# Permuting partitions for a rotary embedding: eight on-chip DMA copies in place of four matrix products

## The chip, the core and the metric

The kernel runs on one NeuronCore of a Trainium2 chip. Its engines are TensorE (PE, with its weight loads as PEld), VectorE (DVE), ScalarE (ACT), GpSimd (POOL) and SyncE (SP). SP only issues DMA transfers here; ACT issues some as well. The metric is the device time of one execution in microseconds (us), taken as the median of several runs.

## The reference, cut to what matters

One layer of a decoder trunk: a normalised input is projected once, the columns of the projection go to four token mixers (A: RWKV-7, B: HGRN2, C: RetNet-style retention, D: RG-LRU), and their outputs are gated, merged and projected back. The change is in branch C, in the rotary embedding of its queries and keys, for 1024 tokens and four heads of 32 channels:

```python
def _rope(t, cos, sin):
    t1, t2 = jnp.split(t, 2, -1)
    return jnp.concatenate([t1 * cos - t2 * sin, t1 * sin + t2 * cos], -1)

def _retention(q, k, v, norm_g):
    ...
    q = _rope(q.astype(jnp.float32).reshape(B, T, H, Dk), cos, sin)
    k = _rope(k.astype(jnp.float32).reshape(B, T, H, Dk), cos, sin) * (Dk ** -0.5)
```

Within a head's 32 channels the first 16 need the second 16 and the other way round. The kernel keeps channels on partitions and tokens along the free dimension, so this is a swap of neighbouring groups of 16 partitions, with a sign.

## The kernel before

The projection is 59 column tiles of 128 columns, in the order of the list `BULK`: four tiles of D, seven of A, then branch C's tiles CQ, CK, CV, CV+1, CG, CG+1, and so on. A tile is computed in split precision: each 128x128 block of weights and each half of 512 tokens takes three products (`hn_hi*w_hi`, `hn_lo*w_hi`, `hn_hi*w_lo`, L591). A tile has two weight halves `p` (0 and 1) and two token halves, so 48 products in four parts of twelve.

Every engine's program is written by hand and runs in order; semaphores tie the engines together. Five places matter.

- **SP (L426 to L449)** loads the weights of tile `bi`, half `p`, into `w_raw[p]` when POOL has split that half of the tile before it (the wait on `s_w_lo_ready`). Its instructions go out strictly in order.
- **POOL (L498 to L509)** splits `w_raw[p]` into `w_hi[p]` and `w_lo[p]`: a cast (L506) and a subtraction (L508). For half 1 of a tile it first waits until PE has finished the tile before.
- **PE (L774 to L813)** runs the tiles. Behind the tile CK (number 12 of `BULK`, counted from 0) come the four products with the table `perm` (L805), a 128x128 signed permutation: q = 0 is the query in `slot(20)`, q = 1 the key in `slot(21)`, each in two token halves, into four PSUM banks. Then come tile 13, the first half of tile 14, and `head_sums(18, 0)` (L797), four products with a block matrix of ones that sum squares over a head for branch A. Ahead of these PE waits for `s_kz_ready`.
- **ACT** copies each finished tile from PSUM to its slot (L1216), and issues the loads of the cosine and sine tables into `slot(16)` and `slot(17)` (L1287, L1288).
- **DVE (L1726 to L1749)** does the rotation: for each of the four 128x512 pieces the permuted piece times sine from PSUM (L1731), the piece itself times cosine in place (L1734), and their sum (L1736). Then it scales the key by a table of decays into `slot(17)` (L1745), which raises `s_kz_ready`, and the query into `slot(16)` (L1748).

```python
            pe.wait_ge(s_gates_ready, 16)
            for q in range(2):
                pe.wait_ge(s_evac, 2 * (BULK_AT[CQ + q] + 1))
                for n in range(2):
                    mm(bank[4 + 2 * q + n][:, :], tb("perm"), ...).then_inc(s_rot_done, 1)
            project(1)
            project_part(0)
            project_part(1)
            pe.wait_ge(s_kz_ready, 1)
            head_sums(18, 0)
```

The wait on `s_kz_ready` is there because the banks 4 to 7 that `head_sums` writes are those that DVE reads in the rotation.

Of the kernel before, what the change touches and what calls it, by code (L numbers as in the profile page):

```python
# [32 lines left out]
P = 128  # L33
T = 1024
# [22 lines left out]
TABLES = (("ident", 128), ("blockones", 128), ("perm", 128), ("xi", 128), ("zeta", 128), ("decay", 512),  # L57
# [42 lines left out]
def build(nc, ins, out_d):  # L100
    x_d, w_mod_d, w_in_d, w_branch_d, w_out_d = (ins[n] for n in ("x", "w_mod", "w_in", "w_branch", "w_out"))
    with ExitStack() as ctx:
# [3 lines left out]
        def sem(name):  # L106
            return ctx.enter_context(nc.semaphore(name))
# [3 lines left out]
        def after(s):  # L111

            counts[s.name] = counts.get(s.name, 0) + 1
            return counts[s.name]
# [48 lines left out]
        s_rot_done = sem("rot_done")  # L163
# [111 lines left out]
        def slot(i):  # L275

            return slots[:, i, :]
# [15 lines left out]
        def tb(name):  # L297
            a, b = TCOL[name]
            return tab[:, a:b]

        def st(a, n):
            return stage[:, a:a + n]
# [21 lines left out]
        rope_tmp = [st(1024, HALF), st(1536, HALF)]  # L324
# [5 lines left out]
        spent = tab[:, TCOL["perm"][0]:TCOL["decay"][1]]  # L330
# [77 lines left out]
        def _(sp):  # L408
# [18 lines left out]
            for bi, ct in enumerate(BULK):  # L427
                if bi < FIRST:
                    continue
                if bi == FIRST:  # L430
                    for src, dst in ((ins["tables"][:, P:], tab[:, P:]), (ins["wa2"], wa2[:, :]),
                                     (ins["reset64"], reset)):
                        sp.dma_start(dst, src).then_inc(s_tables_landed, 16)
                    sp.wait_ge(s_lru_w_zero, 1)
                    for g, name in enumerate(("lru_wa", "lru_wx")):
                        for q in range(4):
                            j, r = q // 2, slice(64 * (q % 2), 64 * (q % 2) + 64)
                            sp.dma_start(lru_w[r, 2 * g + j, r], ins[name][0, q, :, :]).then_inc(
                                s_lru_w_landed, 16)
                for p in range(2):  # L440
# [106 lines left out]
        def _(pe):  # L547
# [254 lines left out]
            for q in range(2):  # L802
                pe.wait_ge(s_evac, 2 * (BULK_AT[CQ + q] + 1))
                for n in range(2):
                    mm(bank[4 + 2 * q + n][:, :], tb("perm"), slot(20 + q)[:, n * HALF:(n + 1) * HALF],  # L805
                       start=True, stop=True).then_inc(s_rot_done, 1)
# [718 lines left out]
        def _(dve):  # L1525
# [5 lines left out]
            def halves(n):  # L1531
                return slice(n * HALF, (n + 1) * HALF)
# [193 lines left out]
            dve.wait_ge(s_rope_landed, 32)  # L1726
            for q in range(2):
                for n in range(2):
                    dve.wait_ge(s_rot_done, 2 * q + n + 1)
                    s = slot(20 + q)[:, halves(n)]  # L1730
                    nc.vector.tensor_tensor(rope_tmp[n], bank[4 + 2 * q + n][:, :], slot(17)[:, halves(n)], MUL)\  # L1731
                        .then_inc(s_vector_step, 1)
                    dve.wait_ge(s_vector_step, after(s_vector_step))
                    nc.vector.tensor_tensor(s, s, slot(16)[:, halves(n)], MUL).then_inc(s_vector_step, 1)  # L1734
                    dve.wait_ge(s_vector_step, after(s_vector_step))
                    nc.vector.tensor_tensor(s, s, rope_tmp[n], ADD).then_inc(s_vector_step, 1)  # L1736
                    dve.wait_ge(s_vector_step, after(s_vector_step))
# [422 lines left out]
def shape_tables():  # L2160
# [6 lines left out]
    perm = np.zeros((P, P))  # L2167
    for m in range(P):
        if m % 32 < 16:
            perm[m + 16, m] = -1  # L2170
        else:
            perm[m - 16, m] = 1
    t["perm"] = perm
# [24 lines left out]
    return {"tables": tables, "cos": np.cos(ang).astype(f), "sin": np.sin(ang).astype(f),  # L2198
# [36 lines left out]
```

## Time and profile before

| | before |
|---|---|
| median of 3 runs | 1105.72 us |
| the three runs | 1106.65, 1105.67, 1105.72 us |
| span of the profiled execution | 1106.6 us |
| PE busy | 1075.6 us (97%) |
| DVE busy | 595.6 us (54%) |
| POOL busy | 375.6 us (34%) |
| ACT busy | 319.9 us (29%) |
| mean granted TensorE clock | 0.996 |

The span is from the first to the last instruction of the profiled execution; of the three runs the 1106.65 us stands next to it, 0.05 us above, and that is what lies around the span. A busy share is an average over stages. The rotation stands at 199 to 218 us of the span, in the stage in which PE streams projection tiles without a pause.

### The profile page before, as it was taken

To read this page: it belongs to the slowest core of one execution; us is meant where nothing else is said; L and a number is where in the kernel's file an instruction comes from. 1 tells how busy PE (TensorE), PEld (TensorE's weight loads), DVE (VectorE), ACT (ScalarE), POOL (GpSimd) and SP (SyncE) were. 2 spreads that over 40 slices of the span, in tenths; PEclk is the share of its full clock that TensorE was granted. 3 is DMA by queue.
4 is the path that set the end of the run, shared out by engine and by line. 5 is a ranking of instruction groups with operands and counts; after the bars stand their busy time and mean duration, and the time that the engine had idled before them with its cause. 6 is when DMAs were issued, how large, how long until landed. Compare 5 with 4: busy or idle time off the path is not lost.

```text
span 1106.6 us, 23043 instructions
## 1 busy us (share of the span) xinstructions
PE 1075.6 (97%) x9992; PEld 830.4 (75%) x9992; DVE 595.6 (54%) x1068; ACT 319.9 (29%) x533; POOL 375.6 (34%) x343
## 2 busy tenths in 40 slices
PE   7999999999999999999999999999999999999997
PEld 5686787767677777777777786877878777887885
DVE  3768933986555332343443118647778587423543
ACT  4545113321521221221221033144545341001221
POOL 1431533312356312212212233244434239762000
PEclk9999999999999999999999999999999999999999
DMA  9700111200100101101111021120101126412221
GB/s 352 259 20 9 48 50 47 76 29 24 40 26 26 49 25 35 40 25 36 37 29 31 28 68 33 44 58 26 50 25 37 39 68 242 143 39 95 95 76 58
DMA packets 80133, 70.28 MB, mean 64 GB/s; under 512 B 4128, under 2 KB 68896, under 8 KB 80032
## 3 DMA queue, kind: packets, MB, share of 16 engines
q1 hardware_dynamic: 74560, 49.34, 14.3%
q10 hardware_dynamic: 5472, 19.47, 4.8%
q8 instruction: 79, 1.29, 0.5%
q14 instruction: 22, 0.18, 0.1%
HBM read 64.60 MB, written 4.19 MB: 62 GB/s over the span
## 4 chain that ended last, share of the span: by engine, by line
PE 88%; DVE 7%; POOL 2%; DMA 1%; ACT 1%; issue 1%; SPq 1%; DVEq 0%; ACTq 0%; POOLq 0%
PE bank L591 53%; PE bank L1104 8%; PE bank L640 8%; PE bank L692 2%; PE bank L1059 1%; DVE slots L1678 1%; PE bank L919 1%; PE bank L915 1%; DMA slots<-in_w_mod 1%; PE bank L797 1%; PE bank L861 1%; PE bank L884 1%; DVE slots L1662 1%; PE bank L972 1%; POOL y_lo L477 1%
## 5 line engine op out<-in xcount | busy, mean ns | idle before, releaser
L591 PE MATMUL bank<-hn_hi,w_hi 128*128 128x512 f32 x880 | 363.0, 412 | 5.8 <-ACT slots L1216 2.3
L591 PE MATMUL bank<-hn_lo,w_hi 128*128 128x512 f32 x880 | 344.4, 391 | 0.0
L591 PE MATMUL bank<-hn_hi,w_lo 128*128 128x512 f32 x880 | 343.8, 391 | 0.0
L506 POOL CAST w_hi<-w_raw 128x512 fp32r<-128x512 f32 x110 | 87.0, 791 | 556.6 <-PE bank L591 556.6
L591 PEld LDWEIGHTS bank<-hn_hi,w_hi 128*128 128x128 f32 x880 | 165.3, 188 | 47.7 <-issue 6.9
L591 PEld LDWEIGHTS bank<-hn_hi,w_lo 128*128 128x128 f32 x880 | 165.6, 188 | 36.4
L591 PEld LDWEIGHTS bank<-hn_lo,w_hi 128*128 128x128 f32 x880 | 165.8, 188 | 32.0 <-issue 1.9
L508 POOL TENSOR_TENSOR w_lo<-w_raw,w_hi 128x512 fp32r<-128x512 f32 x110 | 156.2, 1420 | 8.8
L1238 ACT ACTIVATE stage<-bank 128x512 f32<-128x512 f32 x64 | 37.2, 598 | 160.8 <-PE bank L591 141.9
L1216 ACT ACTIVATE slots<-bank 128x512 f32<-128x512 f32 x42 | 24.6, 598 | 123.0 <-PE bank L591 123.0
L1837 DVE TENSOR_TENSOR stage<-stage,bank 128x512 f32<-128x512 f32 x48 | 33.0, 687 | 49.8 <-PE bank L640 48.6
L640 PE MATMUL bank<-y_hi,w_branch_hi 128*128 128x512 f32 x128 | 53.8, 421 | 0.0
L640 PE MATMUL bank<-y_hi,w_branch_lo 128*128 128x512 f32 x128 | 50.7, 396 | 0.0
L640 PE MATMUL bank<-y_lo,w_branch_hi 128*128 128x512 f32 x128 | 50.5, 395 | 0.0
L1104 PE MATMUL bank<-out_w_hi,hn_hi 128*128 128x512 f32 x128 | 49.9, 390 | 0.2 <-DVE hn_lo L2125 0.2
L1104 PE MATMUL bank<-out_w_lo,hn_hi 128*128 128x512 f32 x128 | 49.8, 389 | 0.0
L1104 PE MATMUL bank<-out_w_hi,hn_lo 128*128 128x512 f32 x128 | 49.8, 389 | 0.0
L1839 DVE TENSOR_TENSOR slots<-slots,stage 128x512 f32<-128x512 f32 x48 | 41.5, 865 | 1.7
L2141 DVE TENSOR_TENSOR fin_tmp<-bank,slots 128x512 f32<-128x512 f32 x16 | 11.1, 692 | 38.2 <-PE bank L1104 38.1
L1924 DVE TENSOR_TENSOR stage<-stage,bank 128x128 f32<-128x128 f32 x32 | 9.2, 287 | 40.5 <-PE bank L919 40.2
L1911 DVE TENSOR_TENSOR stage<-bank,tab 128x128 f32<-128x128 f32 x32 | 9.3, 292 | 38.0 <-PE bank L915 38.0
L518 POOL TENSOR_TENSOR w_branch_lo<-w_branch,w_branch_hi 128x256 fp32r<-128x256 f32 x32 | 28.1, 877 | 2.6
(329 smaller groups left out, 1604.9 us busy)
## 6 DMA issues: line engine op xcount, KB each, us to landing
w_raw<-in_w_in SPq DMA_DIRECT2D x110, 256.0 KB, 2.8
slots<-in_w_mod SPq DMA_DIRECT2D x16, 512.0 KB, 11.4
slots<-in_x SPq DMA_DIRECT2D x8, 512.0 KB, 9.6
w_branch<-in_w_branch SPq DMA_DIRECT2D x32, 128.0 KB, 2.6
slots<-in_w_mod ACTq DMA_DIRECT2D x8, 512.0 KB, 5.4
slots<-in_w_out ACTq DMA_DIRECT2D x8, 512.0 KB, 6.3
xr<-in_x ACTq DMA_DIRECT2D x8, 512.0 KB, 3.5
out<-xr ACTq DMA_DIRECT2D x8, 512.0 KB, 2.6
```

What stands on the lines that cost most here:

```text
L506: nc.gpsimd.tensor_copy(w_hi[p][:, :, :], w_raw[p][:, :, :]).then_inc(s_pool_step, 1)
L508: nc.gpsimd.tensor_tensor(w_lo[p][:, :, :], w_raw[p][:, :, :], w_hi[p][:, :, :].bitcast(F32), ALU.subtract).then_inc(s_w_lo_ready, 1)
L518: nc.gpsimd.tensor_tensor(w_branch_lo[h][:, :, :], w_branch[h][:, :, :], w_branch_hi[h][:, :, :].bitcast(F32), ALU.subtract)\
L591: last = mm(o, w[p][:, k4, :], h[:, k, n * HALF:(n + 1) * HALF], start=(p == 0 and k4 == 0 and q == 0), stop=(p == 1 and k4 == 3 and q == 2))
L640: last = mm(o, w[:, k, :], h[:, k, :], start=(k == 0 and q == 0), stop=(k == 1 and q == 2))
L692: last = mm(bank[q][:, :], w[p][:, k4, cols], h[:, k, n * HALF:(n + 1) * HALF], start=(k == 0 and z == 0), stop=(k == KT - 1 and z == 2))
L1104: last = mm(bank[(2 * tt + n) % 8][:, :], m[tt % 2][:, k * P:(k + 1) * P], w[k][:, n * HALF:(n + 1) * HALF], start=(k == 2 and q == 0), st ...
L1216: nc.scalar.activation(slot(PROJ[ct])[:, halves(n)], src, ACT.Silu if ct in GATED else ACT.Copy).then_inc(s_evac, 1)
L1238: nc.scalar.activation(sig[n], bank[(6 if mi == AHEAD else 0) + n][:, :], ACT.Sigmoid).then_inc(s_evac, 1)
L1837: nc.vector.tensor_tensor(sig[n], sig[n], bank[(4 if mi == AHEAD else 2) + n][:, :], MUL).then_inc(s_vector_step, 1)
L1839: nc.vector.tensor_tensor(o, o, sig[n], ADD).then_inc(s_merged, 1)
L2141: nc.vector.tensor_tensor(tmp, bank[(2 * i + n) % 8][:, :], slot(2)[:, halves(n)], MUL)\
```

## The change

The four products with `perm` and the table itself are gone. In their place SP copies the two slots 20 and 21 within the on-chip memory to a new buffer `rotated` (128 x 2 x 1024, in `stage`), with eight DMA copies of 16 partitions each, 128 KB apiece: group `g` of 16 partitions gets what group `g ^ 1` holds. The copies stand in SP's program ahead of the weight loads of tile 15 and wait until tile CK has been copied out of PSUM. The sign moves into the sine table, on the host. DVE waits for all eight copies (`s_rot_landed` at 128) and then works on whole rows of 1024: six instructions of 128x1024 from on-chip memory in place of twelve of 128x512, four of which read PSUM. `head_sums` still waits for `s_kz_ready`.

```diff
@@ SP
+                if bi == BULK_AT[CK] + 3:
+                    sp.wait_ge(s_evac, 2 * (BULK_AT[CK] + 1))
+                    for g in range(8):
+                        src = slice(16 * (g ^ 1), 16 * (g ^ 1) + 16)
+                        sp.dma_start(rotated[16 * g:16 * g + 16, :, :], slots[src, 20:22, :]).then_inc(s_rot_landed, 16)
                 for p in range(2):
                     if bi > FIRST:
                         sp.wait_ge(s_w_lo_ready, 2 * (bi - FIRST) + p - 1)
@@ PE
             pe.wait_ge(s_gates_ready, 16)
-            for q in range(2):
-                pe.wait_ge(s_evac, 2 * (BULK_AT[CQ + q] + 1))
-                for n in range(2):
-                    mm(bank[4 + 2 * q + n][:, :], tb("perm"), slot(20 + q)[:, n * HALF:(n + 1) * HALF],
-                       start=True, stop=True).then_inc(s_rot_done, 1)
             project(1)
@@ DVE
             dve.wait_ge(s_rope_landed, 32)
+            dve.wait_ge(s_rot_landed, 128)
             for q in range(2):
-                for n in range(2):
-                    dve.wait_ge(s_rot_done, 2 * q + n + 1)
-                    s = slot(20 + q)[:, halves(n)]
-                    nc.vector.tensor_tensor(rope_tmp[n], bank[4 + 2 * q + n][:, :], slot(17)[:, halves(n)], MUL)\
-                        .then_inc(s_vector_step, 1)
-                    dve.wait_ge(s_vector_step, after(s_vector_step))
-                    nc.vector.tensor_tensor(s, s, slot(16)[:, halves(n)], MUL).then_inc(s_vector_step, 1)
-                    dve.wait_ge(s_vector_step, after(s_vector_step))
-                    nc.vector.tensor_tensor(s, s, rope_tmp[n], ADD).then_inc(s_vector_step, 1)
-                    dve.wait_ge(s_vector_step, after(s_vector_step))
+                s, turned = slot(20 + q), rotated[:, q, :]
+                nc.vector.tensor_tensor(turned, turned, slot(17), MUL).then_inc(s_vector_step, 1)
+                after(s_vector_step)
+                nc.vector.tensor_tensor(s, s, slot(16), MUL).then_inc(s_vector_step, 1)
+                dve.wait_ge(s_vector_step, after(s_vector_step))
+                nc.vector.tensor_tensor(s, s, turned, ADD).then_inc(s_vector_step, 1)
+                dve.wait_ge(s_vector_step, after(s_vector_step))
@@ host tables
-    perm = np.zeros((P, P))
...
-    t["perm"] = perm
-    return {"tables": tables, "cos": np.cos(ang).astype(f), "sin": np.sin(ang).astype(f),
+    return {"tables": tables, "cos": np.cos(ang).astype(f), "sin": (np.sin(ang) * np.where(p % 32 < 16, -1, 1)[:, None]).astype(f),
```

SP's program before, from the first weight load of the tile loop to the first load of a branch matrix. `w_raw` is the buffer of a half tile; the 26 loads in one row are those of tiles 5 to 17, two for each.

```order
L438 DMA lru_w<-in_lru_wx 64x64 x4
L448 DMA w_raw<-in_w_in 128x4x128 [waits w4_ready]
L448 DMA w_raw<-in_w_in 128x4x128 [waits gains_ready,w4_ready]
L448 DMA w_raw<-in_w_in 128x4x128 [waits w_lo_ready] x26
L455 DMA w_branch<-in_w_branch 128x2x128
```

The same place of SP's program in the changed kernel (`stage<-slots` are the copies into `rotated`, rows of 2048 elements):

```order
L438 DMA lru_w<-in_lru_wx 64x64 x4
L453 DMA w_raw<-in_w_in 128x4x128 [waits w4_ready]
L453 DMA w_raw<-in_w_in 128x4x128 [waits gains_ready,w4_ready]
L453 DMA w_raw<-in_w_in 128x4x128 [waits w_lo_ready] x20
L444 DMA stage<-slots 16x2048 [waits evac]
L444 DMA stage<-slots 16x2048 x7
L453 DMA w_raw<-in_w_in 128x4x128 [waits w_lo_ready] x6
L460 DMA w_branch<-in_w_branch 128x2x128
```

Twenty loads, those of tiles 5 to 14, stand ahead of the copies; the last of them is half 1 of tile 14. Behind the copies come the loads of tiles 15 to 17.

DVE's program before, from the end of branch A's preparation (L1724) to the query's scaling (L1748):

```order
L1724 COPY slots<-slots 128x1024 [waits vector_step]
L1731 TENSOR_TENSOR stage<-bank,slots 128x512 [waits rot_done,rope_landed,a_b_ready]
L1734 TENSOR_TENSOR slots<-slots 128x512 [waits vector_step]
L1736 TENSOR_TENSOR slots<-slots,stage 128x512 [waits vector_step]
L1731 TENSOR_TENSOR stage<-bank,slots 128x512 [waits rot_done,vector_step]
...
L1745 TENSOR_TENSOR slots<-slots,tab 128x1024 [waits vector_step]
L1748 TENSOR_TENSOR slots<-slots,tab 128x1024 [waits kz_ready]
```

And in the changed kernel:

```order
L1724 COPY slots<-slots 128x1024 [waits vector_step]
L1730 TENSOR_TENSOR stage<-stage,slots 128x1024 [waits rot_landed,rope_landed,a_b_ready]
L1732 TENSOR_TENSOR slots<-slots 128x1024
L1734 TENSOR_TENSOR slots<-slots,stage 128x1024 [waits vector_step]
L1730 TENSOR_TENSOR stage<-stage,slots 128x1024 [waits vector_step]
L1732 TENSOR_TENSOR slots<-slots 128x1024
L1734 TENSOR_TENSOR slots<-slots,stage 128x1024 [waits vector_step]
L1743 TENSOR_TENSOR slots<-slots,tab 128x1024 [waits kz_ready]
```

The first multiplication of the rotation now waits for the copies (`rot_landed`) where it waited for a product of PE (`rot_done`); nothing else has changed its place in DVE's queue.

## Rows read from the trace of the kernel before

**Rows 1.** The page: busy time of each engine, and the chain by engine.

```profile
PE 1075.6 (97%) x9992; PEld 830.4 (75%) x9992; DVE 595.6 (54%) x1068; ACT 319.9 (29%) x533; POOL 375.6 (34%) x343
...
PE 88%; DVE 7%; POOL 2%; DMA 1%; ACT 1%; issue 1%; SPq 1%; DVEq 0%; ACTq 0%; POOLq 0%
```

**Rows 2.** Timeline, PE, around the products with perm: start us, us, engine, line, operation, tiles.

```profile
198.84 0.39 PE L591 MATMUL bank<-hn_hi,w_lo 128*128 128x512 f32 x1
199.06 3.59 PE L805 MATMUL bank<-slots,tab 128*128 128x512 f32 x8
202.09 0.79 PE L591 MATMUL bank<-hn_hi,w_hi 128*128 128x512 f32 x1
202.73 0.39 PE L591 MATMUL bank<-hn_lo,w_hi 128*128 128x512 f32 x1
```

**Rows 3.** Timeline, PE, at the head sums.

```profile
218.84 3.59 PE L797 MATMUL bank<-slots,tab 128*128 128x512 f32 x8
```

**Rows 4.** Timeline, DVE, at the rotation (twelve instructions from 204.84 to 214.07).

```profile
204.11 0.69 DVE L1724 COPY slots<-slots 128x1024 f32<-128x1024 f32 x1
204.84 0.69 DVE L1731 TENSOR_TENSOR stage<-bank,slots 128x512 f32<-128x512 f32 x1
...
214.10 1.52 DVE L1745 TENSOR_TENSOR slots<-slots,tab 128x1024 f32<-128x1024 f32 x1
```

**Rows 5.** Timelines of ACT, POOL and SP, 199 to 203 us.

```profile
199.26 0.60 ACT L1216 ACTIVATE slots<-bank 128x512 f32<-128x512 f32 x1 [1.45 <-PE bank L591]
...
200.34 1.60 POOL L508 TENSOR_TENSOR w_lo<-w_raw,w_hi 128x512 fp32r<-128x512 f32 x1
...
201.96 0.37 SPq L448 DMA_DIRECT2D w_raw<-in_w_in  x1
```

**Rows 6.** Line 455, loads of 128 KB: ns of an issue, and us to landing.

```profile
L455 SPq DMA_DIRECT2D w_branch<-in_w_branch x32: 367/368/647, 256.9 to 982.2; - x32
...
DMA to landing us min/median/max: 2.0/2.6/5.2
```

**Rows 7.** Timeline, SP: one of these loads alone.

```profile
299.97 0.37 SPq L455 DMA_DIRECT2D w_branch<-in_w_branch  x1
```

**Rows 8.** Windows of that load (five of 0.2 us) and of SP's load at 201.96: stretch, busy of the engines, PEclk, DMA share, GB/s.

```profile
300.90:301.10 0.20, 0.20 (x3) 0.15 (x2) 0.20 (x1) 0.00 (x0) 0.00 (x0) 1.00 0.61 131
...
301.70:301.90 0.20, 0.20 (x6) 0.06 (x8) 0.20 (x1) 0.00 (x0) 0.00 (x0) 1.00 0.12 33
...
203.00:204.00 1.00, 1.00 (x6) 0.82 (x5) 1.00 (x1) 0.00 (x0) 0.00 (x0) 1.00 0.75 217
204.00:205.00 1.00, 1.00 (x6) 0.82 (x5) 0.93 (x3) 0.00 (x0) 0.00 (x0) 1.00 0.15 44
```

**Rows 9.** DMA issues: size, us from issue to landing (issued at 193.68 and 194.05).

```profile
w_raw<-in_w_in SPq DMA_DIRECT2D x110, 256.0 KB, 2.8
...
slots<-in_cos ACTq DMA_DIRECT2D x1, 512.0 KB, 3.3
slots<-in_sin ACTq DMA_DIRECT2D x1, 512.0 KB, 4.4
```

**Rows 10.** DVE's groups by line and shape: count, busy us, mean ns.

```profile
L1693 DVE TENSOR_TENSOR slots<-slots 128x1024 f32<-128x1024 f32 x2 | 2.9, 1451 | 0.1
...
L1671 DVE TENSOR_TENSOR slots<-slots 128x1024 f32<-128x1024 f32 x2 | 2.5, 1225 | 0.1
```

**Rows 11.** Timeline, PE, at a wait in branch A's stage.

```profile
619.15 0.50 PE L591 MATMUL bank<-hn_hi,w_hi 128*128 128x512 f32 x1 [1.80 <-DVE slots L1839]
...
620.03 0.63 PE L591 MATMUL bank<-hn_hi,w_hi 128*128 128x512 f32 x1
620.45 0.63 PE L591 MATMUL bank<-hn_lo,w_hi 128*128 128x512 f32 x1
...
623.37 0.40 PE L591 MATMUL bank<-hn_hi,w_lo 128*128 128x512 f32 x1
```

**Rows 12.** Windows behind that wait: stretch, busy of the engines, PEclk, DMA share, GB/s.

```profile
621.00:622.00 1.00, 1.00 (x4) 0.81 (x3) 0.00 (x0) 0.00 (x0) 0.00 (x0) 0.50 0.00 0
```

More of the change, by code:

```diff
@@ L56 @@
           ("conv_b", 2), ("ba", 2), ("bx", 2), ("lam", 2), ("eps", 1), ("ln_eps", 1), ("gamma_c", 1))
-TABLES = (("ident", 128), ("blockones", 128), ("perm", 128), ("xi", 128), ("zeta", 128), ("decay", 512),
+TABLES = (("ident", 128), ("blockones", 128), ("xi", 128), ("zeta", 128), ("decay", 512),
           ("low", NLOW * 32), ("m_rwkv", 128), ("lev", 4 * 32), ("up1", 32), ("eye", 32), ("half", 2), ("ret_head", 4))
@@ L162, in build @@
         s_roots = sem("roots")
-        s_rot_done = sem("rot_done")
+        s_rot_landed = sem("rot_landed")
         s_kz_ready = sem("kz_ready")
@@ L323, in build @@
         kz_tm = st(0, T).rearrange("p (i c) -> p i c", c=P)
-        rope_tmp = [st(1024, HALF), st(1536, HALF)]
+        rotated = st(1024, 2 * T).rearrange("p (q t) -> p q t", q=2)
         ret_p = [st(2048 + 512 * i, 512).rearrange("p (h t) -> p h t", h=4) for i in range(2)]
@@ L328, in build @@
         ret_kv = st(3584, 256)
-        spent = tab[:, TCOL["perm"][0]:TCOL["decay"][1]]
+        spent = tab[:, TCOL["xi"][0]:TCOL["decay"][1]]
         Ep = [a.rearrange("p (g t) -> p g t", t=65) for a in (st(0, 260), spent[:, 0:260])]
@@ L2166, in shape_tables @@
     t["blockones"] = (p[:, None] // 64 == p[None, :] // 64)
-    perm = np.zeros((P, P))
[L2168 to L2172, printed above, removed]
-    t["perm"] = perm
     lg = np.log1p(-np.exp2(-5.0 - np.arange(4)))
```

## The prediction

> **What bounds the kernel now.** I read the page first. PE is busy 97% of the span, and the chain of waits that ended last runs 88% on PE [rows 1]; a microsecond taken from PE's queue is a microsecond of the end, unless PE then waits for something. So the question is where PE stands at each moment around the change, and what it waits for next. The timeline of PE comes next. The four products with the permutation (eight records, since a float32 product is done in two passes) follow tile CK at 199.06, and the second product of the next tile starts at 202.73 [rows 2]; tile 13 and half of tile 14 follow, and the head sums start at 218.84 with no idle time before them [rows 3]. They wait for the key's scaling on DVE, which ends at 214.10 + 1.52 = 215.62 [rows 4], so that wait costs nothing now and has 3.2 us to spare. Last I read when SP, ACT and POOL pass the place at which the copies will stand [rows 5], since the copies are the new input of that chain.
>
> **What is removed.** Products of this stage start 0.22 to 0.23 us apart (198.84, 199.06). Without the four permutation products, the product that now starts at 202.73 would start at 199.06 + 0.23 = 199.29 [rows 2]. That is 3.4 us of PE, all of it on the path, and PE would be at the head sums at 218.84 - 3.4 = 215.4 instead of 218.84 [rows 3]. Tiles 13 and 14 keep their inputs in time: POOL's second half of tile 13 is split by 200.34 + 1.60 = 201.94 [rows 5], and PE needs it after 24 products of 0.23 us, at 204.5.
>
> **What is added: when the copies start.** SP takes its instructions in order, and the last one ahead of the copies is the load of tile 14's second half, issued when POOL is done, at 201.96, for 0.37 us [rows 5]. The wait in front of the copies, for tile CK's copy out of PSUM, is over by then (199.26 + 0.60 = 199.86) [rows 5], so it holds nothing. The first copy is issued at 202.33. At 0.37 us an issue [rows 6] the eighth goes out at 202.33 + 7 x 0.37 = 204.92. The load at 201.96 is ahead of them in the same queue; its 256 KB move from 203 to about 204.2 (217 GB/s in the first microsecond, the rest, 44 KB, in the next) [rows 8]. The copies' own first bytes could come about 0.9 us after the issue, as in the load issued at 299.97 whose bytes begin at 300.9 [rows 7, 8], so 204.2 is where their traffic begins in earnest. Behind the copies SP has tile 15's loads; they wait for POOL's work on tile 14 in any case and are not needed before PE starts tile 15 behind the head sums, so I cost their delay at nothing. Covered by the same argument is the smaller table load at the start, 64 KB less in a queue that nobody waits for at its end.
>
> **How long the copies take.** The trace has no copy within the memory and none of 16 partitions, so this is bounded. The quick end: the sine table's 512 KB, queued behind the cosine's, land at 194.05 + 4.4 = 198.45, against 193.68 + 3.3 = 196.98 for the cosine's [rows 9]; 1.47 us for 512 KB is 0.37 us for 128 KB, just the pace of SP's issues. Then the last copy lands the shortest landing of a 128 KB load behind its issue, 204.92 + 2.0 = 206.9 [rows 6]. The slow end: each copy has to finish before the next does anything, 8 x 2.0 us from 202.33, which is 218.3. Between them, and the row of the same size on the same queue: one 128 KB load alone has its bytes under way from 300.9 to about 301.8, 0.93 us [rows 7, 8]. Eight of those one behind the other are 7.4 us, from 204.2 to 211.6, and landing comes about 0.5 us behind the last bytes (the load of 201.96 lands at 204.76 [rows 5, 9], its bytes end at 204.2), so 212.1. I take this one, because it is the only row of the copies' size, and a copy of few partitions has no reason in the trace to run at the rate of a 512 KB load over all partitions; both ends stay for the range.
>
> The Trainium skill, page "SBUF — State Buffer", section "Door 1: The DMA port swizzle (why `[64,N]` ≈ `[32,N]`)", says that a transfer's rate depends on how many of the memory's sixteen DMA ports its partitions reach, that 16 neighbouring partitions reach four, and gives 104 GB/s for them. By it (an estimate from that figure) a copy would take 1.26 us, the eight would land at 214.8, and the sum below would be +6.8 us in place of +4.1. No row here shows a transfer of 16 partitions.
>
> **DVE.** It ends branch A's preparation at 204.80 [rows 4] and is the engine that the copies now hold: everything behind the first multiplication is queued there, the key's scaling first, for which PE waits. Six multiplications or additions of 128x1024 from on-chip memory take 1.225 us each [rows 10], 7.35 us, with 0.03 us between them 7.5; the same operation took 1.45 us where it met other work [rows 10], so I add 0.2 for one such meeting: 7.8 us, against 214.10 - 204.84 = 9.3 us for the twelve before. The key's scaling adds 1.5 [rows 4]. From landing to the release of PE it is 9.3 us: 212.1 + 9.3 = 221.4.
>
> **The sum.** PE is at the head sums at 215.4 and is released at 221.4: it waits 6.0 us. That is more than the trace shows PE waiting in mid-kernel, and a shorter wait had a second price: after 1.80 us without work at 619.15 the granted clock went to 0.50, that is 1.2 GHz [rows 11, 12], and products started 0.43 us apart (620.03, 620.45) until 623.37; eight of them in 3.34 us instead of 1.8, 1.5 us lost [rows 11]. I count that once. The sum is -3.4 + 6.0 + 1.5 = +4.1 us. Nothing behind it takes it back: DVE's next work (branch A's norms) waits for roots of the head sums themselves, so DVE moves with PE. The profiled execution has a span of 1106.6 us, next to the slowest of the runs (1106.65) and 0.9 above the median, a difference that I leave out of the change: 1106.6 + 4.1 = 1110.7 on its own scale, 1105.7 + 4.1 = 1109.8 us as a median.
>
> **Rivals.**
> - *The copies stream* (faster). They land at 206.9. Then DVE waits 2.1 us, the key is scaled at 216.2, PE waits 0.8 us: -3.4 + 0.8 = -2.6 us, 1103.1. For it: the cosine and sine tables kept that pace over 1 MB [rows 9]. Against it: those are loads over 128 partitions. This decides while the last landing is before 207.3; there PE's wait of 1.2 us still leaves a gain of 2.2. The very best, no wait at all, is -3.4, and needs landing by 206.1, before the 2.0 us of landing are over.
> - *Neighbouring copies overlap two by two* (no change). Copies g and g+1 read and write opposite groups, so that one pair might move in the time of one copy: 204.2 + 4 x 0.93 + 0.5 = 208.4, release at 217.7, PE waits 2.3 us: -1.1 us if the clock holds, +0.4 if it falls, so 1104.6 to 1106.1. For it: several loads share the queue without pauses between them [rows 8, 9]. Against it: all go through one queue in order.
> - *Each copy pays its whole landing* (much slower). Landing at 218.3, release at 227.6: -3.4 + 12.2 + 1.5 = +10.3 us, 1116.0. Against it: the cosine and sine tables did not do that [rows 9].
>
> **How the numbers follow.** Forecast (one behind the other, 0.75 to 1.3 us a copy, which is 1108 to 1113): 50%. Streaming: 22%. Two by two: 20%. Whole landings: 8%. About 0.2%, 2.2 us, is what a measurement of this kernel tells from no change. The boundary to slower is a landing at 210.2 with the clock's fall; a quick end of the forecast, 4%, falls short of it, and 2% of the second rival is a gain. Faster 24%, same 22%, slower 54%. The range goes from the streaming case to the forecast's slow edge, 1103.0 to 1113.5, and leaves out the last rival and the very best case.
>
> **What would show it.** In the changed profile: SP's eight copies issued from 202.3 at 0.37 us each (right start); DVE idle from 204.8 until about 212, ended by a DMA (the copies' time); six instructions of about 1.23 us behind it; PE idle of about 6 us in front of the head sums, ended by DVE; and a granted clock of 0.50 for some 3 us behind that. If DVE's wait ends before 207.3, or PE does not wait at the head sums, the forecast is wrong; if PE waits but its clock stays at 1.00, the sum is 1.5 us too large.

## The result, and the profile after

| kernel | median of the timed runs, us | lowest to highest | span of the profiled execution | its mean granted clock |
|---|---|---|---|---|
| before | 1105.70 (4 runs) | 1104.83 to 1106.65 | 1106.6 | 0.996 |
| changed | 1113.38 (4 runs) | 1112.92 to 1113.63 | 1111.4 | 0.993 |

The change made the kernel slower: ratio 1.0059 (95% interval 1.0043 to 1.0075), 7.7 us between the medians. The run's time is 1.8 us above the span (1113.21 and 1111.4 for the profiled execution), and in every listed run of the two kernels it is 1.75 to 1.86 us above. So the profiled execution of before, with its span of 1106.6, stands for a time of about 1108.4 us (an estimate), 2.7 us above the median. By that distance the run of 1106.65 us is another execution, although the two were put together ahead of the prediction.

The two executions shown so far are 0.8 us apart already ahead of the change: the products of one stage (L786, in after L791) start at 186.7 and 185.9. In a second profile of the kernel before (run 9 below, span 1105.5) they start at 185.9, as after's do. Differences are taken against that one. It puts the head sums at 218.07, the retention's output at 235.8 and the output products at 1010.5; after has 221.63, 241.6 and 1016.3. So +5.8 us arises around the change, and nothing behind it gives it back or adds to it in these two executions.

The page of after, engines and chain, against [rows 1]:

```profile
PE 1074.1 (97%) x9984; PEld 828.9 (75%) x9984; DVE 596.1 (54%) x1062; ACT 319.9 (29%) x533; POOL 374.1 (34%) x343
...
PE 84%; DVE 7%; DMA 3%; POOL 2%; SPq 2%; ACT 1%; issue 1%; DVEq 0%; ACTq 0%; POOLq 0%
```

PE has its eight products fewer (9984 against 9992), and the chain has gone from PE (88% to 84%) to DMA (1% to 3%) and SP's queue (1% to 2%). The timeline of PE, against [rows 2, 3]:

```profile
214.34 0.39 PE L596 MATMUL bank<-hn_hi,w_lo 128*128 128x512 f32 x1
221.63 5.88 PE L802 MATMUL bank<-slots,tab 128*128 128x512 f32 x8 [6.91 <-DVE slots L1743]
226.94 0.79 PE L596 MATMUL bank<-hn_hi,w_hi 128*128 128x512 f32 x1
```

PE is there 3.4 us earlier (idle from 214.72, against 218.07), waits 6.91 us for DVE, and then needs 5.9 us for head sums that took 3.59 [rows 3]. The timeline of DVE, against [rows 4]:

```profile
203.33 0.69 DVE L1724 COPY slots<-slots 128x1024 f32<-128x1024 f32 x1
211.69 1.23 DVE L1730 TENSOR_TENSOR stage<-stage,slots 128x1024 f32<-128x1024 f32 x1 [7.67 <-DMA stage<-slots]
212.83 1.22 DVE L1732 TENSOR_TENSOR slots<-slots 128x1024 f32<-128x1024 f32 x1
214.09 1.22 DVE L1734 TENSOR_TENSOR slots<-slots,stage 128x1024 f32<-128x1024 f32 x1
215.35 1.51 DVE L1730 TENSOR_TENSOR stage<-stage,slots 128x1024 f32<-128x1024 f32 x1
216.78 2.28 DVE L1732 TENSOR_TENSOR slots<-slots 128x1024 f32<-128x1024 f32 x1
219.09 1.23 DVE L1734 TENSOR_TENSOR slots<-slots,stage 128x1024 f32<-128x1024 f32 x1
220.35 1.22 DVE L1743 TENSOR_TENSOR slots<-slots,tab 128x1024 f32<-128x1024 f32 x1
```

It stands still for 7.67 us and then works through, with one instruction of 2.28 us that runs beside POOL's split (POOL's tensor_tensor is busy from 215.86 to 217.98). The copies' line on SP: ns of an issue (min/median/max), first and last start, and landing:

```profile
L444 SPq DMA_DIRECT2D stage<-slots x8: 572/589/717, 201.6 to 206.2; - x8
...
DMA to landing us min/median/max: 3.8/4.7/5.3
```

And windows of this stretch and of PE's wait (busy of the engines, PEclk, DMA share, GB/s):

```profile
204.50:211.50 7.00, 7.00 (x33) 5.79 (x32) 0.00 (x0) 2.48 (x3) 3.29 (x4) 1.00 1.00 147
211.50:212.00 0.50, 0.50 (x4) 0.42 (x3) 0.31 (x1) 0.00 (x0) 0.00 (x0) 1.00 0.03 8
...
219.00:220.00 1.00, 0.00 (x0) 0.00 (x0) 0.96 (x2) 0.00 (x0) 0.00 (x0) 0.61 0.74 209
220.00:221.00 1.00, 0.00 (x0) 0.00 (x0) 0.97 (x2) 0.00 (x0) 0.00 (x0) 0.50 0.18 53
...
225.00:226.00 1.00, 1.00 (x2) 0.34 (x1) 0.00 (x0) 0.55 (x1) 0.00 (x0) 0.50 0.00 0
226.00:227.00 1.00, 1.00 (x5) 0.47 (x3) 0.00 (x0) 0.36 (x2) 0.00 (x0) 0.98 0.00 0
```

The first two windows: 147 GB/s for 7.0 us is 1.03 MB, the eight copies' 1.05 MB; then the traffic is over and DVE goes on. That is 0.87 us a copy, one after the other. The others: the granted clock goes to 0.50 (1.2 GHz) at 219.2, 4.5 us into PE's wait and before its end, and is back at 226 only, so the head sums run at half speed. The chain of after, in order of time (start, us, what), says the same in four steps:

```profile
206.24 5.33 DMA stage<-slots
...
211.69 1.23 DVE stage L1730
...
220.35 1.24 DVE slots L1743
...
221.63 5.88 PE bank L802 x8
```

### The profile page after: what moved, and what is told of

The parts are those of the page before. It is cut to its first block, busy times and chain, and to the rows that moved or that the text cites. A ratio compares the mean times of both kernels' runs of the same rounds, so it can differ in the third digit from the quotient of the medians.

```text
span 1111.4 us, 23025 instructions
## 1 busy us (share of the span) xinstructions
PE 1074.1 (97%) x9984; PEld 828.9 (75%) x9984; DVE 596.1 (54%) x1062; ACT 319.9 (29%) x533; POOL 374.1 (34%) x343
## 4 chain that ended last, share of the span: by engine, by line
PE 84%; DVE 7%; DMA 3%; POOL 2%; SPq 2%; ACT 1%; issue 1%; DVEq 0%; ACTq 0%; POOLq 0%
PE bank L596 52%; PE bank L1104 8%; PE bank L645 8%; PE bank L697 2%; PE bank L1059 1%; DVE slots L1678 1%; PE bank L802 1%; DMA slots<-in_x 1%; PE bank L915 1%; PE bank L919 1%; DMA slots<-in_w_mod 1%; PE bank L861 1%; PE bank L884 1%; DVE slots L1662 1%; PE bank L972 1%
```

## The experiments

Runs 1 to 4 were timed together (before: 1107.83 us), 5 to 8 together (before: 1105.70), 9 to 12 together (before: 1106.57), each series on another chip; a ratio is to the kernel before of its own series. Every experiment starts from the changed kernel unless it says otherwise. "DVE goes on" and the two columns behind it are from the profiled execution; before_again has the output products at 1010.5.

| run | median, us | ratio to before, 95% interval | DVE goes on | PE waits at the head sums | output products |
|---|---|---|---|---|---|
| 1 e1_warm | 1110.76 | 1.0030 (1.0018 to 1.0042) | 211.97 | 0.8 | 1014.0 |
| 2 e2_wide | 1112.46 | 1.0043 (1.0029 to 1.0057) | 208.35 | 4.6 | 1017.5 |
| 3 e3_wait_moved | 1111.77 | 1.0039 (1.0026 to 1.0053) | 211.59 | none; 6.4 later | 1015.9 |
| 4 e4_keys_first | 1108.66 | 1.0011 (1.0002 to 1.0020) | 208.29 | none; 3.1 later | 1010.1 |
| 5 after_again | 1113.86 | 1.0074 (1.0060 to 1.0088) | 210.88 | 6.6 | 1016.2 |
| 6 e6_queries_early | 1105.14 | 0.9990 (0.9982 to 0.9999) | 204.10 | 0.8 | 1008.6 |
| 7 e7_two_queues | 1112.56 | 1.0057 (1.0043 to 1.0070) | 209.73 | 6.2 | 1016.4 |
| 8 e8_order | 1113.87 (1 run) | | 211.40 | 6.6 | 1017.0 |
| 9 before_again | 1107.33 (1 run) | | | none | 1010.5 |
| 10 before_third | 1107.78 (1 run) | | | none | 1010.9 |
| 11 e10_no_copies | 1106.20 | 0.9993 (0.9984 to 1.0003) | 204.38 | 0.8 | 1006.9 |
| 12 e9_both | 1104.09 | 0.9978 (0.9968 to 0.9988) | 204.54 | none | 1008.5 |

**1. e1_warm: the clock's share.** PE is given products with the identity while it would wait.

```diff
+WARM = 28
...
+            for _ in range(WARM):
+                mm(bank[7][:, 0:P], ident, ident, start=True, stop=True)
             pe.wait_ge(s_kz_ready, 1)
             head_sums(18, 0)
```

> The changed kernel with 28 idle products of 128x128 put in front of the head sums, into a bank that nothing uses there, about 6.7 us of work in the 6.9 us that PE waits. Theory (the wait lowers the granted clock and the head sums pay for it): the clock stays at 1.00, the head sums take 3.6 us in place of 5.9, and the time is 2.3 us below the changed kernel, about 1111.1. Rival (the clock is no part of it, the 5.9 us have another cause): head sums as slow as before, time unchanged at 1113.4, or longer by what the products overrun.

Timeline of PE:

```profile
214.70 6.41 PE L812 MATMUL bank<-tab 128*128 128x128 f32 x56
221.91 3.70 PE L803 MATMUL bank<-slots,tab 128*128 128x512 f32 x8 [0.81 <-DVE slots L1746]
225.05 0.80 PE L597 MATMUL bank<-hn_hi,w_hi 128*128 128x512 f32 x1
```

And one window of it:

```profile
220.00:221.00 1.00, 1.00 (x10) 0.92 (x9) 0.97 (x2) 0.00 (x0) 0.00 (x0) 1.00 0.52 155
```

The head sums begin about when they did (221.91 against 221.63), but at full clock: 3.70 us instead of 5.88. The next tile starts at 225.05 instead of 226.94, and the retention's output at 239.8 instead of 241.6. So the clock's share is about 2 us, 2.2 by the duration. The median is 2.9 us above before's of its series, where the changed kernel is 7.7 and 8.2 us above in its own; that is more than the 2.2, and three of the eight runs are at a mean clock of 0.999, too high for a later fall (runs 9 and 10 come back to it).

**2. e2_wide: the copies' shape.** The same bytes in eight copies of 128 partitions by 256 columns, without the permutation, which is left out.

```diff
-                        src = slice(16 * (g ^ 1), 16 * (g ^ 1) + 16)
-                        sp.dma_start(rotated[16 * g:16 * g + 16, :, :], slots[src, 20:22, :]).then_inc(s_rot_landed, 16)
+                        cols = slice(256 * (g % 4), 256 * (g % 4) + 256)
+                        sp.dma_start(rotated[:, g // 4, cols], slot(20 + g // 4)[:, cols]).then_inc(s_rot_landed, 16)
```

> The changed kernel with the eight copies cut the other way: 128 partitions by 256 columns, 128 KB each as before, so the same bytes by the same queue from the same place; they permute nothing (that part of the computation is left out). Theory (16 partitions are what makes a copy slow): the last one lands near 207 in place of 211.6, DVE waits 3 us less or more, PE waits about 2 us, the clock may hold, time 1106 to 1108. Rival (copies within the memory, or eight of 128 KB in one queue, take 1.1 us each however they are cut): landing at 211 to 212, time 1113.4. Second rival (the pace of issue, 0.59 us, sets it): issues still 0.59 us apart and the last landing 2 us behind the last issue, 208.2.

```profile
L444 SPq DMA_DIRECT2D stage<-slots x8: 515/601/611, 201.7 to 206.1; - x8
...
DMA to landing us min/median/max: 2.1/2.1/2.8
```

In this shape a copy lands 2.1 us after its issue, not 4.7, and DVE goes on 3.3 us earlier. Rows over all partitions and the crossing between partitions were changed together, so which of the two counts is not separated; the bytes are not the cause. What is left is the pace of SP's issues, which stays at 0.6 us, as the second rival had it. PE still waits 4.6 us and the clock still falls; and two of DVE's instructions now meet POOL's (2.19 and 2.17 us), which takes a microsecond of the gain.

The late output products of the table are not the copies' doing. The retention's output is at 239.6, 2.0 us ahead of after; behind it PE stands 1.6 us longer in L1059 than in after, in stops that nothing in the profile ends, and after the longest of them the clock falls once more, which it does there in no other profiled execution. This execution is the slowest of the five runs. The stop and the window behind it:

```profile
827.02 0.49 PE L1059 MATMUL bank<-stage 64*32 64x32 f32 x35 [1.42 <-issue]
```

```profile
829.00:830.00 1.00, 1.00 (x4) 0.81 (x3) 0.93 (x4) 0.21 (x1) 0.00 (x0) 0.50 0.00 0
```

**3. e3_wait_moved: where PE waits.** The wait for the scaled key goes from the head sums, which don't read it, to the key's transposes.

```diff
-            pe.wait_ge(s_kz_ready, 1)
             head_sums(18, 0)
...
+            pe.wait_ge(s_kz_ready, 1)
             pe.wait_ge(s_roots, 4)
```

> The changed kernel with PE's wait for the scaled key taken from the head sums (their banks are no longer read by DVE) to the transposes of the scaled key behind tile 14. Theory (PE's 6.9 us and the slow clock come from that wait alone, and DVE is the next limit): no wait at the head sums, which start at 214.6 and run 3.6 us; the transposes come at about 224, when the key is long scaled; but DVE starts branch A's norms only at 224.7, so PE waits some 4 to 5 us at the first retention chunk instead; time 1105 to 1108. Rival (DVE has slack behind it): all 9 us come back, 1104 or less. Second rival (the wait only moves, clock and all): 1111 or more.

The waits, between 230 and 250 us (total, times, longest):

```profile
PE bank L845 <- DVE stage L1789: 6.4, 1, 6.4
```

The wait turns up at the first retention chunk, almost whole, and the clock falls there (0.50 from 235.1 to 245.3). DVE's queue as such is late, not the one wait: the second rival was right.

**4. e4_keys_first: DVE's lateness split.** Copies of one tile each (64 KB), the key's eight first, and DVE rotates and scales the key first (into `rotated`, from where PE transposes it, since the sine table in `slot(17)` is still needed).

```diff
+                    for q in (1, 0):
+                        for g in range(8):
+                            src = slice(16 * (g ^ 1), 16 * (g ^ 1) + 16)
+                            sp.dma_start(rotated[16 * g:16 * g + 16, q, :], slots[src, 20 + q, :]).then_inc(s_rot_landed[q], 16)
...
-            dve.wait_ge(s_rot_landed, 128)
-            for q in range(2):
+            for q in (1, 0):
+                dve.wait_ge(s_rot_landed[q], 128)
...
+                if q == 1:
+                    nc.vector.tensor_tensor(by_chunk(turned), by_chunk(slot(21)), over_chunks("zeta"), MUL)\
+                        .then_inc(s_kz_ready, 1)
```

> Sixteen copies of 64 KB, the key's eight first, the query's eight behind, each with its own semaphore; DVE turns and scales the key as soon as its eight have landed, and PE's wait stays where it is. Theory (a copy's time goes with its bytes at 16 partitions): the key's copies land at about 207.3, the key is scaled by 212.5, PE does not wait at the head sums at 214.6, and the time falls by the 3.4 us of the removed products to about 1102.5. Rival (a copy costs its issue, 0.59 us or more, whatever its bytes): key landed at 209 or later, scaled at 214.2, PE waits a little or not, but the query's copies land at 214 or later and DVE is late with branch A's norms, 1103 to 1106.

A 64 KB copy lands 2.3 us after its issue (2.3/2.3/2.7), all eight keep up with the issues, and DVE starts at 208.29. No wait at the head sums is left; 3.1 us of one appear at a retention chunk, and the median is 0.1% above before:

```profile
235.64 0.71 PE L846 MATMUL bank<-slots,stage 128*128 128x128 f32 x4 [3.05 <-DVE stage L1790]
```

The key's landing lies between the two expectations (207.3 and 209), and the lateness of DVE behind it is the rival's. The time is above both (1102.5, and 1103 to 1106), but before itself is at 1107.83 in this series.

**5. after_again: the changed kernel in the second series.** Unchanged.

> The changed kernel itself, on the chip that also runs the kernels below and the kernel before, since runs of the kernel before have differed by more than 2 us from chip to chip. Theory: 5 to 6 us above the kernel before, which is what the rows of the two traces give from the head sums on (5.05 us, and 0.8 us that the trace of before loses in its first 90 us). Rival: 7.7 us, as the two medians gave on the first chip; then 2 us lie somewhere that the traces do not show.

1113.86 us, 8.2 us over before (interval 6.6 to 9.7). Its trace has the first one's events within 0.8 us (DVE goes on at 210.88, PE waits 6.6 us, the output products start at 1016.2). So the timed difference is larger than the 5.8 us of the traces; runs 9 and 10 take that up.

**6. e6_queries_early: copies ahead of the need.** As in run 4, but the query's eight copies are issued one tile earlier, and DVE keeps its order.

```diff
-                if bi == BULK_AT[CK] + 3:
-                    sp.wait_ge(s_evac, 2 * (BULK_AT[CK] + 1))
+                if bi - BULK_AT[CK] in (2, 3):
+                    q = bi - BULK_AT[CK] - 2
+                    sp.wait_ge(s_evac, 2 * (BULK_AT[CQ + q] + 1))
...
-            dve.wait_ge(s_rot_landed, 128)
+                dve.wait_ge(s_rot_landed[q], 128)
```

> Sixteen copies of 64 KB, with a semaphore for the query and one for the key; the query's eight are issued one tile earlier in SP's program, where SP has some 8 us free, the key's eight where the copies stand now. DVE turns the query first, then the key, as in the changed kernel. Theory (start and bytes of the copies are all that is wrong with the change): query landed long before DVE is free at 204.0, key landed at 208.3, key scaled at 213.4, no wait at the head sums at 214.6, norms of branch A on time, time 3.4 us below the kernel before. Rival (DVE stays late, as with the keys first): a wait of 1 to 3 us at the first retention chunk, time 0.5 to 2.5 us below the kernel before. Second rival (the early copies delay tile 14's weights): PE waits for POOL at tile 14, time equal to before or above.

```profile
204.10 1.61 DVE L1731 TENSOR_TENSOR stage<-stage,slots 128x1024 f32<-128x1024 f32 x1
205.63 2.31 DVE L1733 TENSOR_TENSOR slots<-slots 128x1024 f32<-128x1024 f32 x1
```

DVE has no wait for a copy any more (204.10 follows its copy at 203.37); both tiles' copies are hidden. PE waits 0.8 us, its clock holds there, and the later stages are 2.4 us (retention's output) to 1.9 us (output products) ahead of before_again. The same DVE instruction takes 2.31 us where POOL works beside it, so the key is scaled at 215.5, not at the expected 213.4. The median is only 0.6 us below before (interval 0.1 to 2.0); the expected 3.4 us are not reached, and of the rival the size fits but not its reason, since the waits at the retention chunks are those of before (1.2 us in all).

**7. e7_two_queues: a second queue.** Half of the copies (partitions 64 to 127) issued by ACT at 199.1, half by SP.

```diff
-                    for g in range(8):
+                    for g in range(4):
...
+            act.wait_ge(s_evac, 2 * (BULK_AT[CK] + 1))
+            for g in range(4, 8):
+                src = slice(16 * (g ^ 1), 16 * (g ^ 1) + 16)
+                act.dma_start(rotated[16 * g:16 * g + 16, :, :], slots[src, 20:22, :]).then_inc(s_rot_landed, 16)
```

> The eight copies of the changed kernel split: partitions 64 to 127 issued by ACT as soon as it has copied tile CK out of PSUM (about 199.1), partitions 0 to 63 by SP at the old place (201.6). Theory (each group of partitions has its own limit of about 116 GB/s, so the two halves run beside each other): ACT's four land by about 205, SP's four by 207.5, DVE goes on at 207.5, PE waits about 2.5 us. Rival (the sixteen engines work the copies off one by one from both queues, 1.1 us each): landing at about 209.5, PE waits about 4.5 us, the clock falls.

ACT's four are issued 2.5 us before SP's first, and DVE goes on at 209.73, 2.0 us earlier than in after and 1.2 us earlier than in after_again, so the second queue brought no more than its head start. The window behind SP's load of tile 14, in which copies of both queues move:

```profile
204.50:209.50 5.00, 5.00 (x24) 4.14 (x23) 0.00 (x0) 0.77 (x2) 1.45 (x3) 1.00 1.00 161
```

161 GB/s, with the last of the load in it, is about the 147 of one queue, though SP's copies now land 5.6 us behind their issues. The rate is not the queue's, as the rival had it.

**8. e8_order: neighbours apart.** The order of the copies is 0, 4, 1, 5, 2, 6, 3, 7.

```diff
-                    for g in range(8):
+                    for g in (0, 4, 1, 5, 2, 6, 3, 7):
```

> The eight copies of the changed kernel on SP in the order 0, 4, 1, 5, 2, 6, 3, 7 in place of 0 to 7, so that neighbours in the queue lie in different halves of the partitions. Theory (the limit is one of each group of partitions, and the queue lets neighbours overlap): the issue pace of 0.59 us is the limit, landing at about 208.5 in place of 211.6. Rival (one queue works its copies off in order): landing at 211.6 as before.

DVE goes on at 211.40 against 211.69 and 210.88 with the old order: no difference.

**9 and 10. before_again, before_third: what the traces did not tell.** The kernel before, unchanged, twice.

> The unchanged kernel before, profiled a second time: what the two first traces leave open. They put the change at about +5.9 us where both run the same work, its timed runs at +7.7 and +8.2. Theory: the first profiled execution of before was a slow one of its kind, because its clock fell at 620 us (1.5 us) and it is 0.8 us ahead of the later one only at the start; an execution without that fall has a span near 1104, branch C where it was, and PE without a stretch at 0.50 around 620. Rival: the fall at 620 belongs to every execution of before, the span is 1106 to 1107 again, and the two microseconds are somewhere else.

> The kernel before once more, to see whether the clock's fall at 620 us comes and goes between executions of one kernel. Theory: of the three profiles of before at least one is without it, and the spans differ by about what the fall costs, 1.5 to 2.5 us. Rival: all three have it and the spans agree within 0.5 us.

The expectation failed: both have the fall of [rows 11, 12] at 620 us (spans 1105.5 and 1106.0, clock 0.996), and the rival's 0.5 us between the spans fails too (1106.6, 1105.5, 1106.0). But the timed runs list their clock, and these fall into groups (spans in us; series of runs 5 to 8):

| kernel | clock 0.998 | 0.997 | 0.996 | 0.993 | below |
|---|---|---|---|---|---|
| before | 10 runs, 1103.1 to 1104.0 | 2, 1104.7 and 1104.8 | 3, 1105.5 to 1106.1 | none | none |
| changed | none | none | none | 3, 1111.2 to 1112.1 | 2, 1113.4 and 1113.8 |
| e6_queries_early | 2, 1101.4 and 1102.3 | 3, 1102.4 to 1103.3 | 6, 1102.7 to 1104.6 | none | none |

The fall at 620 lowers the mean clock by 1.7 us of 1105, or 0.0015; the one at the head sums by 3.4 us, or 0.003 (windows summed). Before at 0.996 goes with the first, as in its last two profiled executions, and the changed kernel at 0.993 with both, as in its two: 1105.5 to 1106.1 against 1111.2 to 1112.1, again about 5.9 us. But ten of fifteen runs of before are at 0.998, some 2 us shorter, and none of the nine listed runs of the changed kernel is above 0.994. The missing 2 us are thus a fall that most runs of before in this series did without; that theirs is the one at 620 is inferred from the clock, since no such run was profiled, and run 2 shows that a fall can come at another place too. How often before has one differs between the series: 5 of its 15 runs are at 0.997 or below here, 11 of 18 in the first series and 14 of 23 in the third. That the same stop can go either way is shown. Timeline and window of before_again:

```profile
618.40 0.52 PE L591 MATMUL bank<-hn_hi,w_hi 128*128 128x512 f32 x1 [1.81 <-DVE slots L1839]
```

The window behind it:

```profile
619.00:620.00 1.00, 1.00 (x3) 0.71 (x3) 0.00 (x0) 0.00 (x0) 0.00 (x0) 0.50 0.00 0
```

And of run 4, in which PE stops as long at the same place and the clock stays:

```profile
618.30 0.50 PE L597 MATMUL bank<-hn_hi,w_hi 128*128 128x512 f32 x1 [1.80 <-DVE slots L1838]
```

The window behind it:

```profile
619.00:620.00 1.00, 1.00 (x6) 0.81 (x5) 0.00 (x0) 0.00 (x0) 0.00 (x0) 1.00 0.00 0
```

**11. e10_no_copies: the removed part alone.** Neither products nor copies; the tile itself is multiplied by the sine table, so the permutation is left out.

```diff
-                if bi == BULK_AT[CK] + 3:
...
-            dve.wait_ge(s_rot_landed, 128)
+            dve.wait_ge(s_evac, 2 * (BULK_AT[CK] + 1))
...
-                nc.vector.tensor_tensor(turned, turned, slot(17), MUL).then_inc(s_vector_step, 1)
+                nc.vector.tensor_tensor(turned, s, slot(17), MUL).then_inc(s_vector_step, 1)
```

> Neither products nor copies: the rotation multiplies the tile itself by the sine table where it multiplied the permuted tile, so the permutation is left out. This is the removed part by itself. By the prediction's first term PE gains 3.4 us and reaches the head sums at 214.6; DVE starts the rotation at about 204.1 without a wait and, slowed beside POOL as with the queries copied early, ends the key's scaling at about 215.7, so PE waits about 0.8 us and the clock holds: -2.6 us by the trace. With the theory that before's traced execution is about 2 us above its typical one, the timed runs give 1103.1 to 1105.2, near those with the queries copied early (1105.1). Rival: timed runs show the whole 2.6 us or more (1103.1 or less), so that the early copies themselves cost about 2 us somewhere.

PE is through with its products at 215.05, 3.3 us earlier than in before_again (this execution is 0.3 us behind that one ahead of the change), and waits 0.8, as expected; the retention's output is at 233.7 (235.8 before). The median fell only 0.4 us, within its interval of none. At equal clock the gain is there: at 0.998 and 0.999 four runs span 1102.0 to 1103.1 and nine of before 1103.7 to 1105.2; but four of its eleven runs are at 0.995. Which stretch takes those down was not seen: its one trace has no fall at 620. Neither theory predicted that.

**12. e9_both: runs 3 and 6 together.**

> Queries copied a tile earlier and PE's wait for the key moved from the head sums to the key's transposes. Theory: PE is at the head sums at 214.6 without a wait, the gain over the queries copied early alone is at most the 0.8 us it waited there, 1104.3 to 1105.2, since DVE then holds the first retention chunk, where PE waited 1.2 us. Rival: the whole wait comes back there and the time is that of the queries copied early, 1105.1.

PE starts the head sums with no wait at all, straight behind the last product:

```profile
214.82 0.39 PE L597 MATMUL bank<-hn_hi,w_lo 128*128 128x512 f32 x1
215.05 3.59 PE L803 MATMUL bank<-slots,tab 128*128 128x512 f32 x8
```

1104.09 us, 2.5 us below before, with an interval that excludes no change. It is the fastest version by its median, 0.22% (0.12 to 0.32%) below before; against run 6 it can't be told apart, since the two series had other baselines and their intervals meet.

## Why the prediction was right, and where its size was off

The direction, the mechanism and the order of the events were right, and the time (1113.38) lies just inside the range (to 1113.5), 3.6 us above the forecast of 1109.8. That it lies inside is luck: two of its four runs (1113.56 and 1113.63) and the median of run 5 (1113.86) are above the edge. Step by step, the predicted times moved by the 0.8 us between the two executions:

| step | predicted | measured |
|---|---|---|
| PE earlier at the head sums | 3.4 us | 3.4 us (218.07 to 214.72) |
| first copy issued | 201.5 | 201.6 |
| pace of the issues | 0.37 us | 0.66 us (each takes 0.57 to 0.72) |
| one copy | 0.93 us | 0.87 us |
| last landing | 211.3 | 211.6 |
| DVE, landing to release | 9.3 us | 9.9 us |
| PE's wait | 6.0 us | 6.9 us |
| clock | 1.5 us | 2.3 us |
| sum | +4.1 us | +5.8 us |

**Removed.** Right, and e10 repeats it (3.3 us).

**Landing.** The value taken between the two ends held: eight transfers one behind the other at about the rate of a lone 128 KB load [rows 7, 8]. That 0.87 us came so near to 0.93 is luck in part. The row was taken for its size, and size is not what sets the time: e2's copies have the same size, and over 128 partitions they keep up with issues 0.63 us apart. The issue's pace was wrong, without a consequence here, because the transfers were slower than either pace. The figure of 104 GB/s for 16 partitions (of 1 MiB there) that the prediction cited from the Trainium skill, page "SBUF — State Buffer", section "Door 1: The DMA port swizzle (why `[64,N]` ≈ `[32,N]`)", was too slow for these copies, which moved at 147 GB/s. Its direction agrees: with the same bytes over all partitions a copy landed in 2.1 us. Streaming is refuted by the 7.67 us wait; two by two by the 0.87 us a copy, and by e8 and e7; whole landings by 211.6.

**DVE.** Mis-sized by 0.6 us. The meeting was counted at 0.2 us from the 1.45 us of [rows 10]; beside POOL's split the operation takes 2.28, and one of 1.51 adds to it. The trace of before had this price already, in the query's scaling, which is of the same shape and ran beside POOL's split:

```profile
215.65 2.20 DVE L1748 TENSOR_TENSOR slots<-slots,tab 128x1024 f32<-128x1024 f32 x1
...
214.62 2.15 POOL L508 TENSOR_TENSOR w_lo<-w_raw,w_hi 128x512 fp32r<-128x512 f32 x1
```

**Clock.** The term was taken from a stop of 1.80 us [rows 11], after which 3.3 us of work were slow. Here the clock falls while PE still waits, and the whole of the head sums runs at 1.2 GHz: 5.88 us against 3.59. e1 shows it by itself.

**The step that failed** is the one from the profiled execution to the median: "a difference that I leave out of the change: 1106.6 + 4.1 = 1110.7 on its own scale, 1105.7 + 4.1 = 1109.8 us as a median". It set the span of 1106.6 beside the run of 1106.65 us and so took the profiled execution for one 0.9 us above the median. A run's time is 1.8 us above its span, so that execution is about 2.7 us above: the 0.8 us by which it is late ahead of the change, and a fall of the clock at 620 us worth some 1.7 that not every run has. On the profiled execution's own scale the forecast is thus 1106.6 + 4.1 + 1.8 = 1112.5 us, against 1113.21 measured. The terms that were measured amount to 5.8 us where 4.1 were forecast, and the timed medians differ by 7.7 and 8.2, because the later fall, present in the profiled executions of both, is by the clock in 5 of 15 timed runs of before in the series of runs 5 to 8 and in all nine of the changed kernel. Why it comes more often there stays open. The branch C fall alone doesn't bring it: e3 has that kind of fall and none later, and two of e7's four runs are at 0.995.

## What to carry to other kernels

Moving work from a busy engine to DMA pays only if the data are there when the next engine would have started: here 3.4 us were saved on PE and 6.9 us of waiting bought, since all eight copies stood behind a weight load in SP's queue (first issued at 201.6, with the second tile out of PSUM at 199.0) and DVE waited for the last of them, at 211.6; cut by tile, with the query's issued one tile earlier, they were hidden. Look past the saved engine to the first engine that the transfer holds, and move a wait to where the value is read only after that engine's queue is no longer late (alone it moved the stall, with the early copies it did no harm). A difference between two traces is one between two executions: compare the span of each with the spans and clocks of the timed runs before a microsecond is believed.

## What the runs showed of the hardware that was not expected

- Eight copies within the memory, 16 partitions and 128 KB each, moved at 147 GB/s; their order made no difference, and a second queue left the rate about where it was (161 GB/s). Over 128 partitions, without a permutation, each landed 2.1 us after its issue.
- SP takes 0.57 to 0.83 us to issue such a copy (after, e3, e8), 0.37 us for a load [rows 6]; ACT takes 0.6 us. Half the bytes (64 KB) take as long to issue.
- A DVE tensor_tensor of 128x1024 takes 1.22 us alone and 2.2 to 2.3 beside POOL's tensor_tensor (before, after, e2, e4, e6), and POOL's takes 2.1 in place of 1.3. DVE's end lies near POOL's end plus 1.22 us (217.98 + 1.22 = 219.20, seen 219.06, in after; 206.86 + 1.22 = 208.08, seen 207.94, in e6), as if the later one waited for the other; that it waits is inferred.
- The same stop of 1.8 us at 620 us lowers the clock in some executions (all three profiles of before, both of the changed kernel, e2, e6, e7, e8, e9) and not in others (e1, e3, e4, e10). In e2 one of 1.42 us at 826 does it too; one of 1.45 us at 822 in before_again does not.
